# A decoder block on one core: the convolution's weights on another queue, and the sizes of nine weight fetches

## What is computed

```
h = rms_norm(x, g_mix);  z = h @ w_in + b_in                  # w_in: 1024 x 5376
glu_a, glu_b, q, k, v, gate_conv, gate_attn = split(z)
u = depthwise_causal_conv(glu_a * sigmoid(glu_b), conv_w)     # conv_w: 31 x 1024
y_conv = silu(layer_norm(u + conv_b)) @ w_conv_out + b_conv_out
y_attn = sliding_window_attention(q, k, v, sinks) @ w_attn_out + b_attn_out
x = x + (sigmoid(gate_conv) * y_conv + sigmoid(gate_attn) * y_attn) @ w_out
x = x + moe(rms_norm(x, g_ffn))                               # top 4 of 32 experts,
out = rms_norm(x, g_final)                                    # each w_gate, w_up, w_down: 1024 x 1024
```

## Time and profile before

| | us |
|---|---|
| median of 3 executions | 1160.64 |
| lowest, highest | 1160.05, 1160.66 |
| the profiled execution's own time | 1160.06 |
| its span, first to last instruction | 1158.2 |
| TensorE (PE) busy | 1117.6 |
| VectorE busy | 332.8 |
| ScalarE busy | 177.6 |
| GpSimd busy | 67.4 |

### The profile page before, as it was taken

How to read it: one execution, slowest core, us unless ns; L and a number is a source line. 1 busy time by engine, 2 the same in 40 slices (tenths; PEclk the granted TensorE clock), 3 DMA queues, 4 the chain that set the end, 5 groups by cost and what they waited for, 6 DMA issues and landing times.

```text
span 1158.2 us, 13573 instructions
## 1 busy us (share of the span) xinstructions
PE 1117.6 (96%) x5299; PEld 526.3 (45%) x5299; DVE 332.8 (29%) x795; ACT 177.6 (15%) x351; POOL 67.4 (6%) x67
## 2 busy tenths in 40 slices
PE   8999999999999999999999999999999999999997
PEld 7888888853333333333333333333333333333332
DVE  2999973552111111111111111111111111111111
ACT  2111375221100000001011100100000000000012
POOL 2350013330000000000000000000000000000000
PEclk9999999999999999999999999999999999999999
DMA  9975444689999999999999999999999999999996
GB/s 296 345 222 166 145 164 164 263 345 382 420 429 428 433 432 432 429 432 433 430 433 430 431 432 432 432 431 432 432 429 433 433 432 430 431 431 432 432 424 267
DMA packets 55174, 441.69 MB, mean 381 GB/s; under 512 B 4199, under 2 KB 34153, under 8 KB 38376
## 3 DMA queue, kind: packets, MB, share of 16 engines
q1 hardware_dynamic: 53328, 439.89, 91.5%
q0 software_dynamic: 432, 0.95, 0.4%
q10 hardware_dynamic: 1384, 0.44, 0.2%
HBM read 440.08 MB, written 1.05 MB: 381 GB/s over the span
## 4 chain that ended last, share of the span: by engine, by line
PE 91%; DMA 6%; another core or an unknown queue 2%; DVE 1%; issue 0%; ACT 0%; ACTq 0%; SPq 0%; DVEq 0%
PE bank L1560 55%; PE bank L1303 16%; PE bank L1528 5%; DMA arena<-in_w_down 4%; PE bank L1513 4%; PE bank L1419 2%; PE bank L1596 2%; PE bank L1567 1%; DMA conv_w_rows_then_biases<-in_conv_w 1%; PE bank L1520 1%; PE bank L1603 1%; PE bank L1450 1%; PE bank L1326 1%; PE bank L1351 0%
## 5 line engine op out<-in xcount | busy, mean ns | idle before, releaser
L1560 PE MATMUL bank<-arena,columns_x_block_scatter 128*64 128x512 f32 x3008 | 673.7, 595 | 27.6 <-DMA arena<-in_w_up 18.7
L1560 PEld LDWEIGHTS bank<-arena,columns_x_block_scatter 128*64 128x64 f32 x3008 | 220.6, 137 | 433.3 <-issue 413.2
L1303 PE MATMUL bank<-arena 128*128 128x256 f32 x928 | 203.7, 380 | 1.0 <-DVE arena L869 1.0
L1303 PEld LDWEIGHTS bank<-arena 128*128 128x128 f32 x928 | 175.2, 190 | 26.6 <-issue 2.7
L902 DVE SCALAR_TENSOR_TENSOR arena<-arena x240 | 96.4, 478 | 0.1
L1143 DVE TENSOR_SCALAR bias_selector<-ones_bf,expert_onehot 96x64 bf16<-96x64 bf16 x32 | 7.6, 236 | 267.9 <-PE bank L1520 267.9
L1178 DVE TENSOR_SCALAR gate_clipped<-bank 128x512 f32<-128x512 f32 x32 | 22.1, 692 | 207.4 <-PE bank L1560 207.4
L1182 DVE TENSOR_SCALAR hidden<-bank 128x512 f32<-128x512 f32 x32 | 22.2, 692 | 181.9 <-PE bank L1560 181.9
L1528 PE MATMUL bank<-y_block,columns_x_block_scatter 64*128 64x512 f32 x248 | 61.5, 614 | 0.0
L787 ACT ACTIVATE columns_x_block_scatter<-gate_clipped 128x512 f32<-128x512 f32 x32 | 20.1, 629 | 242.9 <-DVE gate_clipped L1178 242.9
L1513 PE MATMUL bank<-x_normed,select 128*64 128x512 f32 x240 | 56.8, 592 | 0.0
(11 more groups left out here) (207 smaller groups left out, 505.7 us busy)
## 6 DMA issues: line engine op xcount, KB each, us to landing
arena<-in_w_up SPq DMA_DIRECT2D x25, 4096.0 KB, 43.1
arena<-in_w_down SPq DMA_DIRECT2D x25, 4096.0 KB, 44.2
arena<-in_w_gate SPq DMA_DIRECT2D x24, 4096.0 KB, 41.9
arena<-in_w_in SPq DMA_DIRECT2D x20, 1024.0 KB, 11.9
arena<-in_w_gate SPq DMA_DIRECT2D x10, 2048.0 KB, 14.5
arena<-in_w_up SPq DMA_DIRECT2D x9, 2048.0 KB, 15.6
arena<-in_w_down SPq DMA_DIRECT2D x8, 2048.0 KB, 19.1
arena<-in_w_down SPq DMA_DIRECT2D x11, 1024.0 KB, 10.8
```

The lines of the kernel that those rows point to most:

```text
L1303: last = pe.matmul(bank[n % 3][:, j * T:(j + 1) * T], w[:, c, j * P:(j + 1) * P], src[:, c, :], start=(c == 0), stop=(c == C - 1))
L1560: last = pe.matmul(dst[h * CAP:(h + 1) * CAP, :], lhs(row), cols(rows[:, row, :], h), start=(row == 0), stop=(row == MROWS - 1))
```

## The change

Three things. The load of conv_w is taken off ScalarE's queue, where it stood behind the seven vector loads, and issued by SyncE between the second part of w_in's piece 0 and piece 1. Matrices 9 to 11 are fetched in two halves in place of four quarters; their refills then wait for halves, and the single rows of matrices 3 to 5 are not counted any more. Matrices 15 to 17 are fetched whole in place of two halves; the loop that SyncE runs for whole matrices still begins at 18.

```diff
-WHOLES = range(3 * PAIRS, NM - 4)
+WHOLES = range(2 * PAIRS + 3, NM - 4)
...
-for _n in range(7, 2 * PAIRS):
+for _n in range(7, PAIRS + 3):
     ROW_PARTS[_n] = [(0, 2), (2, 4), (4, 6), (6, 8)]
...
-ROWS_USED = {n: (0, 1, 5) if n == 0 else (1, 5) for n in range(PAIRS)}
+ROWS_USED = {n: (0, 1, 5) if n == 0 else (1, 5) for n in range(3)}
...
             sp.dma_start(by_cols(0)[:, rest, :], w_in[:, rest, 0:COLS]).then_inc(slot_full[0], 16)
+            sp.dma_start(cwrows, t_in["conv_w"]).then_inc(cw_loaded, 16)
             for n, col in enumerate(IN_COLS):
...
-            for n in range(PAIRS, WHOLES[0]):
+            for n in range(PAIRS, LOOP0 * PAIRS):
                 for lo, hi in parts_of(n):
                     refill(n, lo, hi)
...
-            act.dma_start(cwrows, t_in["conv_w"]).then_inc(cw_loaded, 16)
```

## The result

| | median us | runs | against before, ratio (95% interval) |
|---|---|---|---|
| before, beside the change | 1160.31 | 17 | |
| the change | 1162.33 | 17 | 1.0017 (1.001 to 1.0023) |

The change is slower by 2.0 us (1.2 to 2.7), just within the 0.2% (2.3 us) that the prediction called no change, though the upper end of the interval is past it, and within its range of 1159.0 to 1162.7. The middle, +0.4 us, was too low. The profiled execution has a span of 1160.2 us against 1158.2.

The account below looks back on a forecast made before the run. TensorE was taken to bound the front and an unpausing fetch stream the rest. A 1.6 us wait less 0.6 us (gap) and 0.6 us (fetch sizes) gave +0.4 us, 1161.0 us, range 1159.0 to 1162.7.

Parts of the forecast that it names:

- What bounds the kernel: Whole kernel: TensorE bounds the first part, then a fetch stream that never pauses, at about 432 GB/s.
- The gap removed: TensorE before the conv_w transposes, near 24 us: the 0.59 us idle goes as conv_w lands earlier, gain 0.6 us.
- The wait for piece 1: TensorE at 16.4 us: conv_w on one engine delays w_in's piece 1 to 18.0 us, costing 1.6 us (1.1 to 2.8).
- The sizes: Fetch stream, matrices 9 to 11 in halves and 15 to 17 whole: gain 0.6 us (0 to 0.8), no pause.
- Hidden: Front: piece 1 isn't late, through engine slack or rows spread on SyncE's queue; -1.2 us, 1159.4 us, chance 0.22.
- No gain from the sizes: Fetch stream: the coarser fetches bring nothing; +1.0 us, 1161.6 us, chance 0.12.
- The clock: TensorE's new gap near 16.4 us: the granted clock falls, 1.7 us lost; +2.1 us, 1162.7 us, chance 0.08.
- Vectors late: Front: vector loads wait for piece 1, end at 20.8 us, their transpose stands 4.5 us; +3.3 us, 1164.0 us, chance 0.11.
- The sum: Whole kernel: +1.6 - 0.6 - 0.6 = +0.4 us on the median, 1161.0 us.

Follow-up runs that it names:

- The quarters: Matrices 12 to 17 fetched in four parts too, in place of halves, against the kernel before: 1161.43 us, ratio 1.0008.
- the wholes: Matrices 9 to 17 each fetched in one piece, conv_w as before, against the kernel before: 1159.30 us, ratio 0.9994.

## Why the prediction was right, and where it was off

**What bounds the kernel.** Right: the expert part runs on one stream of fetches, its start hangs on TensorE's front, and 2.4 us in the front became 2.0 in the end.

**The gap removed, -0.6.** Right in this execution, but the term was too large for a median: the gap was between 0 and 0.6 us in the profiles with conv_w's old place.

**The wait for piece 1, +1.6 (1.1 to 2.8).** Right in place, sign and mechanism, and mis-sized. Piece 1 landed at 19.4, not 18.0. Project(1) began 2.97 us later (19.48 and 16.51), of which 0.22 us are a later project(0): 2.75 us, at the top of the bounds. The step that failed is the choice between the bounds. The earlier trace rows gave 0.22 us a packet, and 31 of them are 6.8 us; the prediction set this aside, for "conv_w won't alternate with w_in on its own queue", and took 5.2. The packets took 7.1 us, 0.23 each. The row was right and the reason against it wrong: conv_w took 7.1 us on SyncE's queue where it had taken 7.8 on ScalarE's, and a packet took 0.17 us for the first seven only (8.9 to 10.1 us).

**The sizes, -0.6 (0 to 0.8).** Right: 0.55 us alone by the medians (its interval doesn't exclude no change), and the landings of that profile gave 0.3 us for 9 to 11 (0.4 against the 29.8 us that the trace's hundredths give for before) and 0.2 for 15 to 17. In the profile of the change a late landing at matrix 15 hid the second, but the late landings add up to much the same in both kernels. The quarters and the wholes, 2.1 us apart, bear the rates out. The stream never paused, as forecast.

**The rivals.** Hidden: it needed the rows spread over engines; two loads made just that, and gave 1159.6 with the sizes where the rival had 1159.4. No gain from the sizes: against it stand the landings and the quarters beside the wholes. The clock: not in the change (no drop in the new gaps); in the move alone the clock did drop at 9.8 us, where it cost nothing behind piece 1. Vectors late: half true. The vectors' packets began at 10.9 us and did not wait for piece 1, but ended later than before, and their transpose waited until 17.4 us; piece 1 came later still. With the vectors 6 us late for a reason of their own the loss was 6.7 us. (That rival's wait is 20.8 - 16.4 = 4.4 us, not 4.5; it changes nothing.)

**The sum.** -0.6 + 2.75 + 0.2 (project(0) later) is 2.4 in the front; less 0.4 won in the stream, from the landing of matrix 8 to that of matrix 17, it is the 2.0 by which the profiled span grew. The first expert matmul came 2.4 us later where the prediction said 1.0.

**What was luck.** The measured +2.0 us is inside the range, but past what the forecast's own sum gives with its upper bound for the wait and the other two terms as forecast (2.8 - 0.6 - 0.6 = +1.6 us). It is the clock's case that took the range up to 1162.7, and the clock did not fall. That the time counts as no change is right for the reason given, a wait set against two small gains, but the wait was four to five times what the gap gave back, and 2.0 us is close to the 2.3 at which it would have been called slower.

## What to carry to other kernels

Before a small load is put in front of a large one, look at how its rows divide: 31 rows passed on one engine and held a 1 MB piece for 6.6 us, where 16 + 15 rows held it for 1.2 to 2.3. A queue in which every piece is awaited hands such a delay to the first piece with less slack than it; two pieces further down it cost nothing. And when the trace has a duration for the thing that is moved, take it, before a reason why it should be shorter.

## What the runs showed of the hardware

A load that sits on one engine holds up its whole queue, not only the piece behind it: SyncE stood 6.4 and 5.9 us in the issues of the next two pieces, against 3.1 and 2.6 us before. It reaches the other queue too: with conv_w in one load on ScalarE's queue SyncE stood 7.8 us in the issue of piece 5 of w_in, with two loads there 4.2 us.

In a full queue the size of a fetch matters little but steadily: 2.48 us for 1 MB, 4.89 for 2 MB, 9.71 for 4 MB, so that a matrix in four parts costs 0.2 us more than whole. A fetch of 4 MB issued 3.6 us before the queue ran out left no pause; one issued 2.0 us before it landed 0.7 us late.
